# Cross attention of a two-layer transformer block: four of eight query chunks between its steps

## The chip, the cores and the metric

The kernel runs on one core of one Trainium2 chip. The core has TensorE (matmul, PE in the profile), VectorE (DVE), ScalarE (ACT), GpSimd (POOL) and SyncE (SP, which issues the DMAs here), each with its own in-order queue, synchronised by semaphores. The metric is the device time of one execution in microseconds.

## The reference, cut to what matters

Two layers, each a mixer of four branches, then cross attention to 256 memory rows, then a gated feed-forward part. `x` is 512 x 1024. The part that matters:

```
def memory_cross_attention(h, mem, mem_norm, wq, wk, wv, wo):
    m = rmsnorm(mem, mem_norm)
    q = (h @ wq).reshape(b, s, 4, 256)
    k = (m @ wk).reshape(b, -1, 4, 256)
    v = (m @ wv).reshape(b, -1, 4, 256)
    sc = einsum('bshd,bmhd->bhsm', q, k) * 256 ** -0.5
    p = softmax(sc, axis=-1)
    o = einsum('bhsm,bmhd->bshd', p, v).reshape(b, s, 1024)
    return o @ wo

x = x + memory_cross_attention(rmsnorm(x, norm_xa), mem, ...)
```

## The kernel before, in words

Activations lie transposed: 128 partitions of features, eight such tiles, 512 tokens along each. A weight matrix is cut into *chunks*: chunk n holds 128 output features of all 1024 inputs. A chunk is loaded as float32 into `raw`, ScalarE rounds it into `wh` (helper `hi(n)`), VectorE takes the rest `raw - wh` into `wl` (helper `lo(n)`), and TensorE multiplies it (helper `gemm`): for each of eight input tiles three fast matmuls of 512 columns, wh with the high part of the activation, wh with its low part, wl with the high part. `raw`, `wh`, `wl` and the PSUM banks `G` have two places each, by n modulo 2. So `hi(n)` waits until chunk n - 2 has been multiplied (`g_full`), `lo(n)` waits for `hi(n)`, `gemm(n)` waits for `lo(n)` and until the bank was emptied by the eviction of chunk n - 2, and SyncE's load of chunk n waits for `lo(n - 2)`.

Chunks N_WQ to N_WQ + 7 make the queries. VectorE evicts each into `qx` (L1289). Their input is the normed `x`, in `a_hi` and `a_lo`. Two query chunks belong to one head.

Cross attention then runs in 11 steps t, each engine through its own loop. Head t // 2, query half t % 2:

- TensorE, t < 8: scores of 256 queries against `kx` in plain float32 (L1716). It first waits until the head's second query chunk is evicted, and for t >= 2 until both exponentials of step t - 2 are done (`e_done` at `48 + 2 * (t - 1)`), which frees the bank.
- VectorE: negated row maximum (L1294), later the reciprocal of the sums (L1298) and the scaling of the exponentials (L1301).
- ScalarE: two exponentials with their sums (L817).
- TensorE, 2 <= t < 10: transposes ("turn") of the probabilities of step t - 2 (L1725); ScalarE copies them into `pt0` or `pt1` (L823).
- TensorE, t = 4, 6, 8, 10: the two output products of head t // 2 - 2, from `vx` and `pt` (L1428, `xo0` to `xo7`); ScalarE and VectorE split them into `b_hi` and `b_lo` (L827, L1306).

Then chunks N_WO to N_WO + 7 (the output projection) follow. No planner is at work: the order in every queue is the order in which the code stands. In VectorE's part the order behind a query chunk is fixed by these lines, the split of the chunk after next ahead of the eviction:

```
lo(n + 2)
...
dve.wait_ge(g_full, n + 1)
dve.scalar_tensor_tensor(qx[:, i, :], G[slot(n % 2)], C_XA, rbc[:], ALU.mult, ALU.mult).then_inc(g_dve, 1)
```

`pt0` and `pt1` lie over the 16 KB of `a_lo`, which nothing reads once the queries are made (L243, L244); `km` (the MLA branch's joined keys, 8 KB) is read by that branch's scores earlier in the layer.

Of the kernel before, what the change touches and what calls it, by code (L numbers as in the profile page):

```python
# [20 lines left out]
F32 = mybir.dt.float32  # L21
# [7 lines left out]
P = 128  # L29
D = 1024  # L30
S = 512
L = 2
KT = D // P
# [16 lines left out]
N_IN, N_WK, N_WV, N_OUT, N_WQ, N_WO, N_UP = 0, 15, 23, 31, 39, 47, 55  # L50
# [74 lines left out]
BIAS_AFTER.update({N_WK - 1 + u: (u,) for u in range(4, 16)})  # L125


def maps_at(t):

    return ([("diff", t, 0), ("diff", t, 1)] if t < 16 else []) + ([("mla", t - 1, 0)] if 1 <= t < 17 else [])  # L130
# [42 lines left out]
def block_program(nc, xT, memT, pos, const, vecs, small, w_first, w_main, w_up, w_down, w_last, out):  # L173
    with ExitStack() as ctx:
# [17 lines left out]
        def sb(name, shape, dt, at=None):  # L192
            size = (2 if dt == BF16 else 4) * int(np.prod(shape[1:]))
            if at is None:
                at = top[0]
                top[0] += (size + 31) // 32 * 32
                assert top[0] <= start + arena_bytes, (name, top[0] - start)
            return nc.alloc_sbuf_tensor_at(name, shape, dt, offset=at), at

        x_sb, _ = sb("x_sb", [P, KT, S], F32)  # L200
        a_hi, a_at = sb("a_hi", [P, KT, S], F32R)
        a_lo, _ = sb("a_lo", [P, KT, S], F32R)
        b_hi, bh_at = sb("b_hi", [P, KT, S], F32R)
        b_lo, bl_at = sb("b_lo", [P, KT, S], F32R)
        mask, _ = sb("mask", [P, 4, S], BF16)
        raw, _ = sb("raw", [P, 2, KT * P], F32)
        wh, _ = sb("wh", [P, 2, KT, P], F32R)
        wl, _ = sb("wl", [P, 2, KT, P], F32R)
        cst, _ = sb("cst", [P, NCC], F32)
        vec, _ = sb("vec", [P, NV], F32)  # L210
        sw, _ = sb("sw", [P, NSW], F32)
        rbc, _ = sb("rbc", [P, S], F32)
        rtmp, _ = sb("rtmp", [P, S], F32)
        rope, _ = sb("rope", [P, S], F32)
        ssum, ssum_at = sb("ssum", [P, S], F32)
        sqx, _ = sb("sqx", [P, 2, S], F32)
        mins, _ = sb("mins", [P, 48], F32)
        sums, _ = sb("sums", [P, 64], F32)
        rec, _ = sb("rec", [P, 64], F32)
        thin, _ = sb("thin", [P, len(ROOTS), 8], F32)  # L220
        xneg, _ = sb("xneg", [P, 16], F32)
        lqk, _ = sb("lqk", [P, 2, 32], F32)
        fvec, _ = sb("fvec", [P, 8], F32)
        lam, _ = sb("lam", [P, 8], F32)
# [15 lines left out]

        mems, _ = sb("mems", [P, KT, 2, M], F32R, a_at)
        memh, meml = mems[:, :, 0, :], mems[:, :, 1, :]
        pt0, _ = sb("pt0", [P, 4, S], F32, a_at + 16384)  # L243
        pt1, _ = sb("pt1", [P, 4, S], F32, a_at + 24576)  # L244
        pt = [pt0, pt1]
        dring, _ = sb("dring", [P, 8, S], F32, a_at + 16384)
        psa, _ = sb("psa", [P, 528], F32, kx_at + 4096)
# [93 lines left out]
        def layer_program(layer):  # L341
# [194 lines left out]
            def scalar(act):  # L536
# [268 lines left out]
                hi(N_WQ + 2)  # L805
                roots("stat_xa", c("eps6"), 1.0 / D)
                row_of("stat_xa")
                for n in range(N_WQ + 1, N_WO):
                    hi(n + 2)

                for t in range(11):
                    if t < 8:
                        act.wait_ge(xmax, t + 1)
                        act.wait_ge(t_full, 32 + t - 3 if t >= 4 else 32)
                        for q in range(2):
                            k = 2 * t + q
                            act.activation(ering[:, t % 4, M * q:M * q + M], SC[t % 2][:, M * q:M * q + M], ACT.Exp,  # L817
                                           bias=xneg[:, k:k + 1], accum_out=sums[:, 48 + k:49 + k]).then_inc(e_done, 1)
                    if 2 <= t < 10:
                        u = t - 2  # L820
                        act.wait_ge(t_full, 32 + u + 1)
                        act.wait_ge(v_full, V_AT[("diff1", "diff1", "xo1", "xo3")[u // 2]] + 1)
                        act.activation(pt[u // 2 % 2][:, 0:2, M * (u % 2):M * (u % 2) + M],  # L823
                                       TR[u % 2].rearrange("p (k q) -> p k q", k=2), ACT.Copy).then_inc(t_free, 1)
                    if t >= 4 and t % 2 == 0:
                        for i in range(t - 4, t - 2):
                            act.activation(b_hi[:, i, :], v_wait(f"xo{i}"), ACT.Copy).then_inc(o_hi, 1)  # L827
# [64 lines left out]
            def vector(dve):  # L892
# [386 lines left out]
                        lo(N_OUT + i + 2)  # L1279
                    split_x(i, mix, v("g_xa", i))  # L1280

                for i in range(KT):
                    n = N_WQ + i
                    lo(n + 2)
                    if i == 0:
                        inverse("stat_xa")
                        row_in("stat_xa")
                    dve.wait_ge(g_full, n + 1)
                    dve.scalar_tensor_tensor(qx[:, i, :], G[slot(n % 2)], C_XA, rbc[:], ALU.mult, ALU.mult).then_inc(g_dve, 1)  # L1289

                for t in range(11):
                    if t < 8:
                        dve.wait_ge(s_full, 48 + t + 1)
                        dve.tensor_reduce(xneg[:, 2 * t:2 * t + 2], SC[t % 2].rearrange("p (q m) -> p q m", q=2),  # L1294
                                          AX.X, ALU.max, negate=True).then_inc(xmax, 1)
                        k = 48 + 2 * t
                        dve.wait_ge(e_done, k + 2)
                        step(dve.reciprocal(rec[:, k:k + 2], sums[:, k:k + 2]))  # L1298
                        for q in range(2):
                            e = ering[:, t % 4, M * q:M * q + M]  # L1300
                            ins = dve.tensor_scalar(e, e, rec[:, k + q:k + q + 1], None, ALU.mult)  # L1301
                        ins.then_inc(p_ready, 1)
                    if t >= 4 and t % 2 == 0:
                        for i in range(t - 4, t - 2):
                            dve.wait_ge(o_hi, i + 1)
                            dve.tensor_tensor(b_lo[:, i, :], v_wait(f"xo{i}"), b_hi[:, i, :].bitcast(F32),  # L1306
                                              ALU.subtract).then_inc(v_dve, 1)
# [73 lines left out]
            def tensor(pe):  # L1381
# [23 lines left out]
                def gemms(base, count, his, los, tokens, free, tiles=range(KT), lead=0):  # L1405

                    turns = (count - lead) // 4 if count - lead > 6 else 0
                    for s in range(lead, count - 4 * turns):
                        gemm(base + s, (base + s) % 2, his, los, tokens, free, tiles)
                    if turns:  # L1410
                        at = base + count - 4 * turns
                        with pe.Fori(0, turns) as j:
                            for s in range(4):
                                gemm(j * 4 + at + s, (at + s) % 2, his, los, tokens, free, tiles)
# [285 lines left out]
                gemm(N_WQ + 1, 0, a_hi, a_lo, free="wq", tiles=range(4), end=False)  # L1700
                row_of("stat_xa")
                gemm(N_WQ + 1, 0, a_hi, a_lo, tiles=range(4, KT), begin=False)
                gemms(N_WQ, KT, a_hi, a_lo, S, "wq", lead=2)

                for t in range(11):
                    if t < 8:
                        h, qp = t // 2, t % 2
                        pe.wait_ge(g_dve, g_dve_count(N_WQ + 2 * h + 1, "wq"))
                        if t >= 2:
                            pe.wait_ge(e_done, 48 + 2 * (t - 1))  # L1710
                        else:
                            pe.wait_ge(s_seen, 48)
                        for q in range(2):
                            at = (2 * qp + q) * P
                            for i in range(2):
                                last = pe.matmul(SC[t % 2][:, M * q:M * q + M], qx[:, 2 * h + i, at:at + P],  # L1716
                                                 kx[:, 2 * h + i, :], start=(i == 0), stop=(i == 1))
                        last.then_inc(s_full, 1)
                    if 2 <= t < 10:
                        u = t - 2  # L1720
                        pe.wait_ge(p_ready, 16 + u + 1)
                        pe.wait_ge(t_free, 32 + u - 1)
                        for q in range(2):
                            for m in range(2):
                                last = pe.transpose(TR[u % 2][:, M * m + P * q:M * m + P * q + P],  # L1725
                                                    ering[:, u % 4, M * q + P * m:M * q + P * m + P], ident)
                        last.then_inc(t_full, 1)
                    if t >= 4 and t % 2 == 0:
                        h = t // 2 - 2
                        pe.wait_ge(t_free, 32 + 2 * h + 2)  # L1730
                        for i in range(2):
                            product(f"xo{2 * h + i}", *[(vx[:, m, GW * h + P * i:GW * h + P * i + P],
                                                         pt[h % 2][:, m, :]) for m in range(2)])

                gemm(N_WO, 1, b_hi, b_lo, free="wo",
                     ready=lambda i: pe.wait_ge(v_dve, V_FREED["dve"].index(f"xo{i}") + 1))
# [203 lines left out]
```

## Time and profile before

| | us |
|---|---|
| median of 3 runs (lowest, highest) | 1634.95 (1634.67, 1635.6) |
| the profiled execution, its own time | 1632.93 |
| its span, first to last instruction | 1631.1 |
| TensorE matmuls busy | 1580.3 |
| VectorE busy | 1009.3 |
| ScalarE busy | 729.4 |
| GpSimd busy | 166.7 |
| mean granted clock of TensorE, as a share of 2.4 GHz | 0.986 |

The span lies inside the execution's own time; the remaining 1.8 us are before and after it. Busy times of engines overlap, so they do not add up to the span. Matmuls are pipelined: one that is shown with 0.39 us is followed by the next after 0.23 us, so prices are read from one start to the next.

### The profile page before, as it was taken

What the parts mean: (1) busy time and instruction counts of PE and PEld (TensorE: products, weight loads), DVE (VectorE), ACT (ScalarE), POOL (GpSimd) and SP (SyncE); (2) the same over time, 40 slices, a digit from 0 to 9 for tenths busy, and PEclk for the clock granted to TensorE, in tenths of its full rate; (3) what the DMA queues carried; (4) which work ended last, traced back from release to release, by engine and by line L of the source; (5) the groups of instructions that cost most, each with busy time, mean ns of one, the idle gap of its engine ahead of it and who ended that gap; (6) DMA issues with size and microseconds to landing.
All of it is one profiled execution on the core that took longest, in us unless ns stands there. A gap on an engine that the chain in (4) does not pass through costs nothing.

```text
span 1631.1 us, 21918 instructions
## 1 busy us (share of the span) xinstructions
PE 1580.3 (97%) x7934; PEld 1236.5 (76%) x7934; DVE 1009.3 (62%) x1565; ACT 729.4 (45%) x1137; POOL 166.7 (10%) x114
## 2 busy tenths in 40 slices
PE   6999899999999999999999999999999999999997
PEld 3774677687688888888888677768768888888886
DVE  6785976443447746745767997654344773674574
ACT  5785667432444423423453266743244441442342
POOL 0000024220030000000021402422003000000002
PEclk9998999999999999999999999999999999999998
DMA  5321432122022223232233133212202223222222
GB/s 185 117 91 46 149 104 98 52 91 91 13 91 95 98 91 103 90 104 90 90 141 114 65 104 110 98 52 91 91 13 91 103 90 103 91 103 91 98 82 91
DMA packets 45438, 151.31 MB, mean 93 GB/s; under 512 B 5040, under 2 KB 5296, under 8 KB 44720
## 3 DMA queue, kind: packets, MB, share of 16 engines
q1 hardware_dynamic: 45360, 150.24, 26.6%
q8 instruction: 53, 0.87, 0.2%
q14 instruction: 25, 0.20, 0.0%
HBM read 142.88 MB, written 7.34 MB: 92 GB/s over the span
## 4 chain that ended last, share of the span: by engine, by line
PE 91%; DVE 5%; ACT 2%; issue 1%; DMA 1%; SPq 0%; DVEq 0%; ACTq 0%
PE psum L1395 25%; PE psum L1397 25%; PE psum L1398 25%; PE psum L1428 4%; PE psum L1583 2%; PE psum L1594 2%; PE psum L1561 2%; PE psum L1569 2%; PE psum L1463 1%; PE psum L1437 1%; PE psum L1449 1%; DVE wl L899 1%; ACT wh L543 1%; DVE acc L941 1%; PE psum L1716 1%
## 5 line engine op out<-in xcount | busy, mean ns | idle before, releaser
L543 ACT ACTIVATE wh<-raw 128x1024 fp32r<-128x1024 f32 x226 | 239.4, 1059 | 577.5 <-PE psum L1398 563.8
L1395 PE MATMUL psum<-a_hi,wh 128*128 128x512 f32 x1072 | 426.0, 397 | 0.8 <-DVE a_lo L964 0.6
L1397 PE MATMUL psum<-a_lo,wh 128*128 128x512 f32 x1072 | 419.8, 392 | 0.0
L1398 PE MATMUL psum<-a_hi,wl 128*128 128x512 f32 x1072 | 419.5, 391 | 0.0
L899 DVE TENSOR_TENSOR wl<-raw,wh 128x1024 fp32r<-128x1024 f32 x222 | 272.7, 1228 | 128.7 <-ACT wh L543 128.5
L1395 PE MATMUL psum<-b_hi,wh 128*128 128x512 f32 x608 | 240.9, 396 | 8.2 <-DVE x_sb L1273 4.4
L1395 PEld LDWEIGHTS psum<-a_hi,wh 128*128 128x128 f32 x1072 | 203.1, 189 | 51.0 <-issue 5.4
L1398 PE MATMUL psum<-b_hi,wl 128*128 128x512 f32 x608 | 237.6, 391 | 0.0
L1397 PE MATMUL psum<-b_lo,wh 128*128 128x512 f32 x608 | 237.3, 390 | 0.0
L1398 PEld LDWEIGHTS psum<-a_hi,wl 128*128 128x128 f32 x1072 | 202.8, 189 | 42.9
L1397 PEld LDWEIGHTS psum<-a_lo,wh 128*128 128x128 f32 x1072 | 203.1, 189 | 42.3 <-issue 1.2
L1273 DVE TENSOR_TENSOR x_sb<-x_sb,psum 128x512 f32<-128x512 f32 (+1 forms) x80 | 54.9, 686 | 180.2 <-PE psum L1398 180.2
L1395 PEld LDWEIGHTS psum<-b_hi,wh 128*128 128x128 f32 x608 | 114.6, 188 | 37.6 <-issue 6.5
L1397 PEld LDWEIGHTS psum<-b_lo,wh 128*128 128x128 f32 x608 | 114.6, 188 | 24.0 <-issue 1.0
L1398 PEld LDWEIGHTS psum<-b_hi,wl 128*128 128x128 f32 x608 | 114.4, 188 | 24.2
L925 DVE TENSOR_TENSOR up<-psum,rbc 128x512 f32<-128x512 f32 x88 | 60.9, 692 | 89.2 <-PE psum L1398 84.5
L941 DVE SCALAR_TENSOR_TENSOR acc<-conv_in,vec,acc 128x512 f32<-128x512 f32 x120 | 95.6, 797 | 3.4
L517 POOL TENSOR_TENSOR ssum<-ssum,sqx 128x512 f32<-128x512 f32 x41 | 73.1, 1784 | 128.7 <-ACT sqx L566 128.7
L1395 PE MATMUL psum<-mems,wh 128*128 128x256 f32 x256 | 81.3, 318 | 0.0
L504 POOL TENSOR_TENSOR wl<-raw,wh 128x1024 fp32r<-128x1024 f32 x20 | 47.9, 2393 | 322.2 <-ACT wh L543 320.9
L514 POOL COPY ssum<-sqx 128x512 f32<-128x512 f32 x6 | 4.3, 719 | 720.3 <-ACT sqx L566 720.3
L1397 PE MATMUL psum<-mems,wh 128*128 128x256 f32 x256 | 72.7, 284 | 0.0
(223 smaller groups left out, 1953.3 us busy)
## 6 DMA issues: line engine op xcount, KB each, us to landing
raw<-in_w_main SPq DMA_DIRECT2D x106, 512.0 KB, 3.2
raw<-in_w_up SPq DMA_DIRECT2D x88, 512.0 KB, 3.2
raw<-in_w_down SPq DMA_DIRECT2D x32, 512.0 KB, 3.2
raw<-in_w_last SPq DMA_DIRECT2D x16, 384.0 KB, 3.0
bias_scratch<-ptr SPq DMA_DIRECT2D x16, 256.0 KB, 2.8
bias<-bias_scratch SPq DMA_DIRECT2D x16, 256.0 KB, 3.8
sw<-in_small SPq DMA_DIRECT2D x2, 1152.0 KB, 6.3
raw<-in_w_first SPq DMA_DIRECT2D x4, 512.0 KB, 4.9
```

The source lines that it names most:

```text
L504: pool.tensor_tensor(wl[:, slot(n % 2)].rearrange("p k m -> p (k m)"), raw[:, slot(n % 2), :], wh[:, slot(n % 2)].rearrange("p k m -> p (k ...
L517: pool.tensor_tensor(ssum[:], ssum[:], sqx[:, k % 2, :], ALU.add).then_inc(ss_in, 1)
L543: act.activation(wh[:, slot(b)].rearrange("p k m -> p (k m)")[:, 0:width], raw[:, slot(b), 0:width], ACT.Copy).then_inc(w_hi, 1)
L899: dve.tensor_tensor(wl[:, slot(b)].rearrange("p k m -> p (k m)"), raw[:, slot(b), :], wh[:, slot(b)].rearrange("p k m -> p (k m)").bitcast ...
L925: dve.tensor_tensor(dst, G[slot(b)], rbc[:], ALU.mult).then_inc(g_dve, 1)
L941: ins = dve.scalar_tensor_tensor(acc[:, i, :], win, w, acc[:, i, :], ALU.mult, ALU.add)
L1273: dve.tensor_tensor(x_sb[:, at, :], x_sb[:, at, :], G[slot(b)].rearrange("p (o s) -> p o s", o=1), ALU.add).then_inc(g_dve, 1)
L1395: pe.matmul(out_ap, wh[:, slot(b), k, :], his[:, k, :], start=((begin or first) and i == 0), stop=False)
L1397: pe.matmul(out_ap, wh[:, slot(b), k, :], los[:, k, :], start=False, stop=False)
L1398: last = pe.matmul(out_ap, wl[:, slot(b), k, :], his[:, k, :], start=False, stop=(end and i == len(tiles) - 1))
L1428: last = pe.matmul(ps[rows, cols], lhs, rhs, start=(i == 0), stop=(i == len(pairs) - 1))
L1561: pe.matmul(SC[m], qk[rows, h // 2, qb * P:qb * P + P], qk[rows, 2 + h // 2, :], start=True, stop=True).then_inc(s_full, 1)
```

## The change

The queries' first four chunks are multiplied as before, ahead of the attention steps. The last four stand in the steps: TensorE multiplies query chunk 4 at the end of step 2, 5 at the end of step 3, 6 at the end of step 4, 7 at the end of step 5. ScalarE's conversion of the chunk after next and VectorE's split and eviction stand at the beginning of steps 3, 4, 5 and 6. Because `a_hi` and `a_lo` are now read until step 5, `pt0` and `pt1` (which use only two of their four planes) shrink to two planes each and lie over `km`.

```diff
--- before.py
+++ after.py
@@ -123,6 +123,10 @@
 STORES_AHEAD = {n: (n - 4,) for n in range(4, 16)}
 STORES_AHEAD.update({16: (12, 13, 14), 17: (15,)})
 BIAS_AFTER.update({N_WK - 1 + u: (u,) for u in range(4, 16)})
+
+
+
+XA_CHUNKS = {3: 4, 4: 5, 5: 6, 6: 7}
 
 
 def maps_at(t):
@@ -240,8 +244,8 @@
 
         mems, _ = sb("mems", [P, KT, 2, M], F32R, a_at)
         memh, meml = mems[:, :, 0, :], mems[:, :, 1, :]
-        pt0, _ = sb("pt0", [P, 4, S], F32, a_at + 16384)
-        pt1, _ = sb("pt1", [P, 4, S], F32, a_at + 24576)
+        pt0, _ = sb("pt0", [P, 2, S], F32, km_at)
+        pt1, _ = sb("pt1", [P, 2, S], F32, km_at + 4096)
         pt = [pt0, pt1]
         dring, _ = sb("dring", [P, 8, S], F32, a_at + 16384)
         psa, _ = sb("psa", [P, 528], F32, kx_at + 4096)
@@ -805,10 +809,12 @@
                 hi(N_WQ + 2)
                 roots("stat_xa", c("eps6"), 1.0 / D)
                 row_of("stat_xa")
-                for n in range(N_WQ + 1, N_WO):
+                for n in range(N_WQ + 1, N_WQ + 4):
                     hi(n + 2)
 
                 for t in range(11):
+                    if t in XA_CHUNKS:
+                        hi(N_WQ + XA_CHUNKS[t] + 2)
                     if t < 8:
                         act.wait_ge(xmax, t + 1)
                         act.wait_ge(t_full, 32 + t - 3 if t >= 4 else 32)
@@ -1279,7 +1285,8 @@
                         lo(N_OUT + i + 2)
                     split_x(i, mix, v("g_xa", i))
 
-                for i in range(KT):
+                def queries(i):
+
                     n = N_WQ + i
                     lo(n + 2)
                     if i == 0:
@@ -1288,7 +1295,12 @@
                     dve.wait_ge(g_full, n + 1)
                     dve.scalar_tensor_tensor(qx[:, i, :], G[slot(n % 2)], C_XA, rbc[:], ALU.mult, ALU.mult).then_inc(g_dve, 1)
 
+                for i in range(4):
+                    queries(i)
+
                 for t in range(11):
+                    if t in XA_CHUNKS:
+                        queries(XA_CHUNKS[t])
                     if t < 8:
                         dve.wait_ge(s_full, 48 + t + 1)
                         dve.tensor_reduce(xneg[:, 2 * t:2 * t + 2], SC[t % 2].rearrange("p (q m) -> p q m", q=2),
@@ -1700,7 +1712,8 @@
                 gemm(N_WQ + 1, 0, a_hi, a_lo, free="wq", tiles=range(4), end=False)
                 row_of("stat_xa")
                 gemm(N_WQ + 1, 0, a_hi, a_lo, tiles=range(4, KT), begin=False)
-                gemms(N_WQ, KT, a_hi, a_lo, S, "wq", lead=2)
+                gemm(N_WQ + 2, 1, a_hi, a_lo, free="wq")
+                gemm(N_WQ + 3, 0, a_hi, a_lo, free="wq")
 
                 for t in range(11):
                     if t < 8:
@@ -1731,6 +1744,9 @@
                         for i in range(2):
                             product(f"xo{2 * h + i}", *[(vx[:, m, GW * h + P * i:GW * h + P * i + P],
                                                          pt[h % 2][:, m, :]) for m in range(2)])
+                    if t + 1 in XA_CHUNKS:
+                        i = XA_CHUNKS[t + 1]
+                        gemm(N_WQ + i, (N_WQ + i) % 2, a_hi, a_lo, free="wq")
 
                 gemm(N_WO, 1, b_hi, b_lo, free="wo",
                      ready=lambda i: pe.wait_ge(v_dve, V_FREED["dve"].index(f"xo{i}") + 1))
```

## Rows read from the trace of the kernel before

**Rows 1.** The page: busy time of TensorE, and the weight loads (size, us to landing).

```profile
PE 1580.3 (97%) x7934; PEld 1236.5 (76%) x7934; DVE 1009.3 (62%) x1565; ACT 729.4 (45%) x1137; POOL 166.7 (10%) x114
...
raw<-in_w_main SPq DMA_DIRECT2D x106, 512.0 KB, 3.2
```

**Rows 2.** Windows of the stage: length, busy us and instructions of each engine, granted clock (PEclk).

```profile
399.88:436.28 36.40, 32.16 (x130) 21.30 (x128) 17.70 (x41) 18.35 (x49) 0.00 (x0) 1.00 0.04 15
424.05:436.28 12.23, 10.04 (x38) 5.67 (x36) 4.15 (x9) 4.87 (x11) 0.00 (x0) 1.00 0.00 1
1172.65:1209.04 36.39, 32.15 (x130) 21.29 (x128) 17.70 (x41) 18.35 (x49) 0.00 (x0) 1.00 0.04 15
```

**Rows 3.** Timeline of TensorE, first layer: start, us, then idle before it and its releaser.

```profile
399.88 3.61 PE L1716 MATMUL psum<-kx,qx 128*128 128x256 f32 x16
404.84 1.97 PE L1716 MATMUL psum<-kx,qx 128*128 128x256 f32 x8 [1.35 <-ACT ering L817]
406.65 0.60 PE L1725 MATMUL psum<-cst,ering 128*128 128x128 f32 x4
...
416.29 1.89 PE L1716 MATMUL psum<-kx,qx 128*128 128x256 f32 x8
418.01 0.60 PE L1725 MATMUL psum<-cst,ering 128*128 128x128 f32 x4
418.45 1.89 PE L1716 MATMUL psum<-kx,qx 128*128 128x256 f32 x8
...
420.62 3.60 PE L1428 MATMUL psum<-pt,vx 128*128 128x512 f32 x8
424.05 1.89 PE L1716 MATMUL psum<-kx,qx 128*128 128x256 f32 x8
...
428.26 3.70 PE L1428 MATMUL psum<-pt,vx 128*128 128x512 f32 x8 [1.45 <-ACT pt L823]
...
436.28 0.80 PE L1395 MATMUL psum<-b_hi,wh 128*128 128x512 f32 x1
```

**Rows 4.** Timelines of ScalarE and VectorE behind the last query chunk, first layer.

```profile
394.69 1.06 ACT L543 ACTIVATE wh<-raw 128x1024 fp32r<-128x1024 f32 x1 [4.38 <-PE psum L1398]
400.13 1.06 ACT L543 ACTIVATE wh<-raw 128x1024 fp32r<-128x1024 f32 x1 [4.38 <-PE psum L1398]
...
401.22 1.22 DVE L899 TENSOR_TENSOR wl<-raw,wh 128x1024 fp32r<-128x1024 f32 x1 [3.61 <-ACT wh L543]
402.37 0.68 DVE L1289 SCALAR_TENSOR_TENSOR qx<-psum,rbc 128x512 f32<-128x512 f32 x1
402.96 0.68 DVE L1294 TENSOR_REDUCE xneg<-psum 128x2 f32<-128x512 f32 x1
```

**Rows 5.** Windows over gaps of TensorE elsewhere, and over what followed them.

```profile
129.20:132.50 3.30, 0.00 (x0) 0.00 (x0) 0.69 (x1) 3.24 (x4) 0.00 (x0) 1.00 0.46 174
133.50:147.20 13.70, 13.70 (x37) 3.60 (x37) 4.82 (x8) 0.00 (x0) 0.00 (x0) 0.50 0.01 1
195.30:197.50 2.20, 0.00 (x0) 0.00 (x0) 2.16 (x5) 0.01 (x1) 0.00 (x0) 1.00 0.60 212
198.40:201.80 3.40, 3.40 (x17) 3.24 (x15) 3.33 (x8) 1.92 (x5) 0.00 (x0) 0.50 0.00 0
321.30:324.70 3.40, 3.40 (x9) 2.62 (x9) 2.69 (x4) 2.08 (x3) 1.91 (x2) 0.51 0.30 116
1092.30:1094.50 2.20, 0.01 (x2) 0.04 (x1) 1.89 (x3) 0.69 (x3) 0.00 (x0) 1.00 0.00 0
1096.00:1100.00 4.00, 4.00 (x19) 3.34 (x18) 2.38 (x3) 1.77 (x3) 2.16 (x2) 1.00 0.36 125
```

**Rows 6.** Timeline around one such gap, at the start of the output chunks.

```profile
319.28 0.68 DVE L1273 TENSOR_TENSOR x_sb<-x_sb,psum 128x512 f32<-128x512 f32 x1
...
320.11 0.48 PE L1395 MATMUL psum<-b_hi,wh 128*128 128x512 f32 x1 [2.20 <-DVE x_sb L1273]
...
320.42 0.40 PE L1397 MATMUL psum<-b_lo,wh 128*128 128x512 f32 x1
```

## Prediction

> **What bounds the kernel now.** I read the page first: TensorE's matmuls are busy 97% of the span [rows 1]. A change that adds no arithmetic can therefore only win where TensorE waits or where its clock is down, and it loses wherever it makes TensorE wait. Then I read the stage that the diff touches, from the first cross-attention score to the first matmul of the output projection: 36.40 us in the first layer and 36.39 us in the second, all at granted clock 1.00 [rows 2]. The two copies agree, so I work out one layer and double it.
>
> The timeline of TensorE through the stage [rows 3] gives the price of each piece by differences of starts. A step's scores take 418.01 - 416.29 = 1.72 us, its transposes ("turn") 418.45 - 418.01 = 0.44 us, a pair of output products 424.05 - 420.62 = 3.43 us. Eight scores, eight turns and four pairs make 31.0 us, so TensorE idles 5.4 us here. Three parts: 1.35 us before the scores of step 2, which wait for the first exponentials; small gaps from step 2 to step 6, where the chain maximum, exponential, reciprocal takes longer than the matmuls; and the tail after the scores of step 7, 12.23 us long, with 1.45 us of its wait in one row.
>
> How much is in the middle part? From the turn in step 2 (406.65) to the scores of step 7 (424.05) are 17.40 us. The matmuls there are five turns, four scores and two pairs: 2.20 + 6.88 + 6.86 = 15.94 us. The gaps are 1.46 us.
>
> **What the change moves.** Four query chunks of 24 matmuls leave the front of the stage and stand at the ends of steps 2, 3, 4 and 5. A chunk costs 400.13 - 394.69 = 5.44 us of TensorE, read from one weight conversion to the next [rows 4]; 4 x 5.44 = 21.76 us stand in both kernels and cancel. The opening stays: scores 0 and 1, the split and eviction behind the last chunk, the table load and the 1.35 us wait follow chunk 3 as they followed chunk 7. The tail stays too: the last chunk is over before step 6, and between scores 6 and scores 7 stand the same turn and pair. Nothing fills the 1.45 us there.
>
> **What it wins.** From step 3 on each score finds its exponentials done, since a chunk of 5.44 us stands before it. All the middle gaps go: -1.46 us a layer. The cover holds even though ScalarE and VectorE now do a weight conversion, a weight split and an eviction before the maximum of steps 3 and 5. That maximum starts about 3.1 us after its chunk's end (402.96 against 399.88 for the same three pieces in the old order [rows 3, 4]) and its probabilities are ready some 2.6 us later, 5.7 us in all; TensorE has scores, turn and the next chunk to do, 1.72 + 0.44 + 5.44 = 7.6 us.
>
> **What it costs: two waits.** The scores of steps 4 and 5 belong to head 2, which reads query chunks 4 and 5. The wait in front of step 4 asks for chunk 5 evicted, and chunk 5 is the very last thing TensorE did, at the end of step 3. The same holds for chunk 7 before step 6. Chunks 4 and 6 are not wanted at once and cost nothing. What lies between the end of a chunk and its eviction is seen behind chunk 7 of the old order [rows 4]: ScalarE converts the weights of the chunk after next (it has to wait for this chunk, whose buffer it overwrites) from 400.13, VectorE splits them from 401.22, and only then, because `lo(n + 2)` stands ahead of the eviction in `queries`, the eviction runs from 402.37 to 403.05. In the old order this was hidden behind scores 0 and 1 (3.44 us), which read other chunks. Now nothing is behind the waiting scores but what they must precede: TensorE's queue is in order, so the turn, the pair and the next chunk wait too.
>
> The size: TensorE's next slot would be 399.88 [rows 3]; the eviction ends at 403.05; from the end of a VectorE instruction to the matmul that it frees are 320.11 - (319.28 + 0.68) = 0.15 us [rows 6]. So 403.20 - 399.88 = 3.32 us, and the first matmul after an idle stretch takes 0.31 us to its successor [rows 6] instead of a chunk's usual 5.44 / 24 = 0.23, 0.08 us. That is 3.40 us a wait, 6.80 us a layer.
>
> **Small terms.** Each chunk now follows other matmul forms and may pay that same 0.08 us again: between 0 and 0.32 us a layer; I take 0.32, the nearest row. The number of instructions of every engine is the same; the loop of chunks was already written out. SyncE's weight loads keep their order and come later with the splits that free their buffers: a load lands in 3.2 us [rows 1] and is issued behind the split of two chunks before, which is at least 8 us ahead of the conversion that reads it (two chunks less the 2.5 us of conversion and split), so 0. GpSimd has nothing in this stage. The turned tiles `pt0` and `pt1` move to the place of `km`, last read in the maps before; they keep their waits, so 0.
>
> Per layer: 6.80 + 0.32 - 1.46 = +5.66 us; two layers +11.3 us.
>
> **The clock.** These are gaps of over 3 us, which the stage did not have. Elsewhere the trace has four gaps of 2.2 to 3.3 us in the middle of work [rows 5, 6]. After an idle 2.2 us the granted clock fell to 0.50 (1.2 of 2.4 GHz) at 198.4 for 3.4 us; after an equal one that ended at 320.1 it fell at 321.3 for 3.4 us; after 3.3 us of idle it fell for 13.7 us, in products that partly use half the rows; a third gap of 2.2 us, at 1092.3, did not bring it down. So three of four fell, the longest among them. I take three of my four waits to be followed by one such stretch. A stretch costs half of 3.4 us, 1.7 us, since dense matmuls stand behind both waits: +5.1 us. The bounds are nothing, and for all four two stretches each, 13.6 us.
>
> The Trainium skill, "TensorE: Matmul & The Clock Gate", section "HAM oscillation", says that waits between bursts of matmuls bring the array back to the lower clock and that every following burst then starts slow. By that rule all four waits would be followed by a slow stretch and the clock term would be 6.8 us, for a sum of +18.1 us. The trace agrees in three gaps of four.
>
> **The sum.** +11.3 + 5.1 = +16.4 us. The profiled execution took 1632.93 us (span 1631.1), which would become 1649.3; the median of the runs shown is 2.0 us above it, and 1634.95 + 16.4 = 1651.4 us is my forecast, 1.0% slower.
>
> **The rivals.**
> *The waits are there, the clock holds.* For it: the gap at 1092.3 left the clock at 1.00. Against it: my gaps are half again as long. +11.3 us, 1646.3 us, down to 1645.2 without the small term and with 0.1 us less a wait. Chance 0.2.
> *The clock stays down longer.* For it: the 13.7 us stretch; scores, turn and pair behind the wait are plain fp32 as the products there were. Against it: those products partly used 64 rows, and in the other two cases one stretch was enough. Two stretches behind each wait: 11.3 + 13.6 = +24.9 us, 1659.9 us. Chance 0.09.
> *The eviction is not held back by the split.* If the wait were only chunk end to eviction, 0.25 + 0.68 + 0.15 + 0.08 = 1.16 us, the layer would be 2.32 + 0.32 - 1.46 = +1.2 us, and the kernel 1637.3 us, within 0.2%. Against it stands the order in `queries` and the row of the split. Chance 0.05.
> *The gaps are filled and no new wait opens* (the other side). This asks that the evictions of chunks 5 and 7 are done when the scores come. It decides below (1.46 - 0.32) / 2 = 0.57 us a wait. With none, the layer wins 1.14 us: 1632.7 us, still within 0.2%; only with the opening wait and the tail filled too (5.4 us of idle less 0.32, twice) could it reach -10.2 us, 1624.8 us. For it: the gaps are real and a chunk is long enough. Against it: chunks 5 and 7 directly precede their readers, and neither opening nor tail is touched. Chance 0.06, half of it faster.
>
> **How the numbers follow.** Forecast 0.60, for one to four ordinary slow stretches (1648.0 to 1653.1 us); clock holds 0.20; longer stretches 0.09; small wait 0.05; no wait 0.06. The range runs from the clock-holds case, with a microsecond below it, to just short of the case of two stretches everywhere: 1644 to 1659 us. It leaves out the two unslowed cases and the far end of the long stretches, some 0.15. A measurement of this kernel tells 0.2%, 3.3 us, from no change. Faster 0.03, within 0.2% 0.07, slower 0.90.
>
> **What the profile after would show.** Right: two rows in each layer where the scores wait over 3 us for VectorE's `qx`, a stage from first score to output projection of 36.4 + 21.8 + 5.7 = 63.8 us plus clock losses, no wait at steps 3 and 5, the same tail, and a clock of 0.50 behind most waits. Wrong: a wait near 1 us would mean that the split does not hold the eviction back; waits at steps 3 or 5 that my cover of 7.6 us was miscounted; a tail shorter than 12.2 us that I missed what the new order does late.

## The result, and the profile after

| | before | after |
|---|---|---|
| median, us | 1634.95 | 1649.31 |
| lowest to highest of 5 runs, us | 1631.89 to 1637.43 | 1646.89 to 1650.88 |
| ratio to before, 95% interval | | 1.0096 (1.0085 to 1.0108) |
| profiled execution (span), us | 1632.93 (1631.1) | 1650.88 (1649.1) |

The changed kernel is about 1% slower; the forecast was 1651.4 us. From the page of the changed kernel, the row that answers to [rows 1]: the same 7934 matmuls, 7.0 us more of recorded busy time.

```profile
PE 1587.3 (96%) x7934; PEld 1240.1 (75%) x7934; DVE 1015.3 (62%) x1565; ACT 729.9 (44%) x1137; POOL 163.9 (10%) x114
```

Windows of the changed kernel answer to [rows 2]: the stage from the first score to the first output matmul, in both layers, and the tail of the first from the scores of step 7. The columns are those of [rows 2].

```profile
379.17:444.37 65.20, 55.52 (x225) 40.22 (x224) 25.08 (x49) 22.74 (x53) 0.00 (x0) 0.97 0.12 41
1159.03:1225.94 66.91, 57.23 (x225) 41.38 (x224) 25.10 (x49) 22.80 (x53) 0.00 (x0) 0.95 0.12 40
432.15:444.37 12.22, 10.03 (x37) 5.66 (x36) 4.03 (x8) 4.87 (x11) 0.00 (x0) 1.00 0.00 0
```

The stage now holds four chunks more, 21.76 us. Against 36.40 and 36.39 us it grew by 28.80 and 30.52 us, so it lost 7.04 and 8.76 us, 15.8 us together, of 18.0 us between the two profiled spans. The tail is 12.22 us, as before (12.23). Where the 15.8 us are is seen in the timeline of TensorE, which answers to [rows 3]; the chunks' own matmuls are left out.

```profile
379.17 3.61 PE L1729 MATMUL psum<-kx,qx 128*128 128x256 f32 x16
384.14 1.97 PE L1729 MATMUL psum<-kx,qx 128*128 128x256 f32 x8 [1.36 <-ACT ering L823]
385.94 0.60 PE L1738 MATMUL psum<-cst,ering 128*128 128x128 f32 x4
...
391.85 1.89 PE L1729 MATMUL psum<-kx,qx 128*128 128x256 f32 x8
...
402.71 1.99 PE L1729 MATMUL psum<-kx,qx 128*128 128x256 f32 x8 [3.07 <-DVE qx L1296]
...
413.89 1.89 PE L1729 MATMUL psum<-kx,qx 128*128 128x256 f32 x8
...
424.76 3.55 PE L1729 MATMUL psum<-kx,qx 128*128 128x256 f32 x8 [3.07 <-DVE qx L1296]
428.10 0.77 PE L1738 MATMUL psum<-cst,ering 128*128 128x128 f32 x4
428.71 3.60 PE L1440 MATMUL psum<-pt,vx 128*128 128x512 f32 x8
432.15 1.89 PE L1729 MATMUL psum<-kx,qx 128*128 128x256 f32 x8
...
436.36 3.70 PE L1440 MATMUL psum<-pt,vx 128*128 128x512 f32 x8 [1.45 <-ACT pt L829]
```

The middle gaps are gone: nothing waits before the scores at 391.85 (step 3) and 413.89 (step 5). Two waits of 3.07 us took their place, at 402.71 (step 4) and 424.76 (step 6), both released by VectorE's `qx`. What VectorE did before the first of them answers to [rows 4]:

```profile
400.83 1.23 DVE L905 TENSOR_TENSOR wl<-raw,wh 128x1024 fp32r<-128x1024 f32 x1 [3.31 <-ACT wh L547]
401.97 0.68 DVE L1296 SCALAR_TENSOR_TENSOR qx<-psum,rbc 128x512 f32<-128x512 f32 x1
404.75 0.69 DVE L1306 TENSOR_REDUCE xneg<-psum 128x2 f32<-128x512 f32 x1 [2.09 <-PE psum L1729]
```

It splits weights from 400.83, evicts chunk 5 from 401.97 to 402.65, and TensorE starts at 402.71. The next slot after chunk 5 would have been at 399.49 (its last matmul started at 399.26), so the wait is 3.22 us long. The view of waits, over both layers, adds the four up:

```profile
PE psum L1729 <- DVE qx L1296: 12.3, 4, 3.1
```

The scores at 424.76 took 3.55 us where eight usually take 1.89. That is the granted clock, in these windows behind the four waits:

```profile
402.70:406.00 3.30, 3.29 (x15) 2.55 (x16) 0.69 (x1) 0.53 (x3) 0.00 (x0) 1.00 0.44 159
425.10:428.50 3.40, 3.40 (x11) 2.65 (x10) 0.15 (x1) 0.00 (x0) 0.00 (x0) 0.51 0.47 159
1183.00:1186.00 3.00, 3.00 (x8) 2.25 (x7) 0.00 (x0) 0.00 (x0) 0.00 (x0) 0.50 0.50 175
1206.80:1210.10 3.30, 3.30 (x11) 2.57 (x10) 0.27 (x1) 0.00 (x0) 0.00 (x0) 0.50 0.45 159
```

Three of four waits were followed by a stretch at 0.50 to 0.51, 1.2 of 2.4 GHz; the first wait of the first layer was not.

Outside the stages 2.2 us remain. Half of it is in front of the first stage, which would begin at 378.12 if only four chunks had left and begins at 379.17; the other half is in the last rows of the program. There VectorE's last residual and its first output stood 6.78 us apart in the changed kernel, 5.78 before, with only small matmuls between them:

```profile
1634.27 0.69 DVE L1279 TENSOR_TENSOR x_sb<-x_sb,psum 128x512 f32<-128x512 f32 x1 [3.39 <-PE psum L1410]
...
1641.05 5.35 DVE L1819 SCALAR_TENSOR_TENSOR x_sb<-x_sb,vec,psum 128x512 f32<-128x512 f32 x8 [2.23 <-PE psum L1461]
```

```profile
1617.34 0.69 DVE L1273 TENSOR_TENSOR x_sb<-x_sb,psum 128x512 f32<-128x512 f32 x1 [3.39 <-PE psum L1398]
...
1623.12 5.36 DVE L1803 SCALAR_TENSOR_TENSOR x_sb<-x_sb,vec,psum 128x512 f32<-128x512 f32 x8 [1.90 <-PE psum L1449]
```

The change has nothing in either place; the clock was down at other moments there. In front of the stage the granted clock was 0.51 from 35.9 to 42.8 us (0.75 before), 0.81 from 98 to 107 us (0.62 before) and 0.54 from 131 to 149.5 us (0.63 before). At the end it fell to 0.50 at 1636.8 us, half way through the small matmuls; before it fell at 1621.8 us, in their last group.

### The profile page after: what moved, and what is told of

The parts are those of the page before. It is cut to its first block, busy times and chain, and to the rows that moved or that the text cites. A ratio compares the mean times of both kernels' runs of the same rounds, so it can differ in the third digit from the quotient of the medians.

```text
span 1649.1 us, 21918 instructions
## 1 busy us (share of the span) xinstructions
PE 1587.3 (96%) x7934; PEld 1240.1 (75%) x7934; DVE 1015.3 (62%) x1565; ACT 729.9 (44%) x1137; POOL 163.9 (10%) x114
## 4 chain that ended last, share of the span: by engine, by line
PE 91%; DVE 5%; ACT 2%; issue 1%; DMA 1%; SPq 0%; DVEq 0%; ACTq 0%
PE psum L1407 25%; PE psum L1410 24%; PE psum L1409 24%; PE psum L1440 4%; PE psum L1595 2%; PE psum L1606 2%; PE psum L1573 2%; PE psum L1729 2%; PE psum L1581 2%; DVE wl L905 1%; PE psum L1475 1%; PE psum L1449 1%; ACT wh L547 1%; PE psum L1461 1%; DVE acc L947 1%
## 5 line engine op out<-in xcount | busy, mean ns | idle before, releaser
L1410 PEld LDWEIGHTS psum<-a_hi,wl 128*128 128x128 f32 x1072 | 202.6, 189 | 42.8
```

The costliest lines, as they stand in the source:

```text
L1410: last = pe.matmul(out_ap, wl[:, slot(b), k, :], his[:, k, :], start=False, stop=(end and i == len(tiles) - 1))
```

## The experiments

One theory stood against three rivals. Theory W: the loss is two waits a layer, each the length of conversion, split and eviction of a chunk that the very next scores read, and a slow clock behind most of them. The rivals: the place of the tiles costs (M), interleaving costs in itself (I), the clock costs nothing and the waits are all of it (C). All kernels were timed against the kernel before on the same chip; those of the first four experiments shared one chip, the next three another, the last two a third. The median of before was 1634.66, 1633.21 and 1633.5 us on these chips.

**The tiles moved, nothing else.**

```diff
-        pt0, _ = sb("pt0", [P, 4, S], F32, a_at + 16384)
-        pt1, _ = sb("pt1", [P, 4, S], F32, a_at + 24576)
+        pt0, _ = sb("pt0", [P, 2, S], F32, km_at)
+        pt1, _ = sb("pt1", [P, 2, S], F32, km_at + 4096)
```

> The kernel before with one half of the change alone: the turned tiles pt0 and pt1 lie over km, the order of all queues is as before. Theory W (two waits per layer of some 3.2 us in front of the scores of steps 4 and 6, and a slow clock behind most of them) expects no change: within 0.2% of 1635 us, a stage of 36.4 us in each layer. Rival M (the place of the tiles costs: ScalarE's copies into them or the output products that read them are slower there) expects the copies above 0.60 us or the products' pairs above 3.43 us, and part of the 14 us lost.

1635.13 us, ratio 1.0003 (0.9991 to 1.0015). The stages, as windows:

```profile
399.76:436.17 36.41, 32.16 (x130) 21.31 (x128) 17.70 (x41) 18.36 (x49) 0.00 (x0) 1.00 0.05 16
1174.15:1210.56 36.41, 32.16 (x130) 21.30 (x128) 17.70 (x41) 18.35 (x49) 0.00 (x0) 1.00 0.05 15
```

ScalarE's copies into `pt` took 0.59 us each, as in the kernel before. This half of the change costs nothing; rival M is out.

**The eviction ahead of the split**, for the four moved chunks of the changed kernel:

```diff
-                    lo(n + 2)
+                    if not evict_first:
+                        lo(n + 2)
...
                     dve.scalar_tensor_tensor(qx[:, i, :], ...).then_inc(g_dve, 1)
+                    if evict_first:
+                        lo(n + 2)
...
-                        queries(XA_CHUNKS[t])
+                        queries(XA_CHUNKS[t], evict_first=True)
```

> The changed kernel, with the eviction of the four moved chunks ahead of the weight split in VectorE's queue. Theory W expects the two waits per layer to fall from an idle of 3.07 us to about 0.8 us (0.25 to VectorE's start, 0.68 for the eviction, 0.06 to TensorE, less the 0.16 us that a matmul's record outlasts its slot), some 2.25 us less each, and the slow clock behind them to vanish: 1649.3 - 4 x 2.25 - 5 = about 1635.5 us, the same as the kernel before. Rival I (interleaving itself costs, by switches between matmul forms and by ScalarE and VectorE being late everywhere) expects it to stay above 1645 us.

1634.36 us, ratio 1.0007 (0.9994 to 1.0020). VectorE's timeline before step 4, first layer, and the two waiting scores of that layer in TensorE's:

```profile
399.74 0.69 DVE L1297 SCALAR_TENSOR_TENSOR qx<-psum,rbc 128x512 f32<-128x512 f32 x1 [2.75 <-PE psum L1413]
400.89 1.23 DVE L905 TENSOR_TENSOR wl<-raw,wh 128x1024 fp32r<-128x1024 f32 x1 [0.46 <-ACT wh L547]
```

```profile
400.49 1.99 PE L1732 MATMUL psum<-kx,qx 128*128 128x256 f32 x8 [0.78 <-DVE qx L1297]
...
420.24 1.99 PE L1732 MATMUL psum<-kx,qx 128*128 128x256 f32 x8 [0.78 <-DVE qx L1297]
```

The stages of both layers, as windows:

```profile
379.20:438.17 58.97, 53.86 (x225) 39.08 (x224) 25.47 (x49) 22.66 (x53) 0.00 (x0) 1.00 0.14 46
1155.30:1214.27 58.97, 53.86 (x226) 39.07 (x224) 25.47 (x49) 22.66 (x53) 0.00 (x0) 1.00 0.14 45
```

One exchange of two instructions on VectorE gives back all of the loss that can be measured. The waits are 0.78 us each instead of 3.07, and the granted clock is 1.00 through both stages. The stage takes 58.97 us, 0.8 us more than the 58.16 us of the old order with four chunks in it (36.40 + 21.76): the short waits cost a little more than the filled gaps give, too little for the medians to show. Rival I is out: the chunks are still between the steps. The Trainium skill, "TensorE: Matmul & The Clock Gate", section "Architectural detail: the array is 16× 32×32, not 1× 128×128", says that VectorE and ScalarE take their instructions strictly in order. The trace agrees: in the changed kernel the eviction, whose input was ready at the chunk's end (399.49), ran only behind the split, at 401.97; here it ran at 399.74.

**Each moved chunk one step earlier.**

```diff
-XA_CHUNKS = {3: 4, 4: 5, 5: 6, 6: 7}
+XA_CHUNKS = {2: 4, 3: 5, 4: 6, 5: 7}
```

> The changed kernel with each moved chunk one step earlier (ends of steps 1, 2, 3 and 4), so that chunks 5 and 7 have a whole step between them and the scores that read them. Theory W expects no wait for the evictions at all, and also the opening wait of 1.36 us filled, as a chunk now stands in front of the scores of step 2: per layer 1.46 + 1.36 + 0.08 saved less up to 0.2 for switches, so the stage is 58.16 - 2.7 = 55.4 us from the first score with four chunks in it, and the kernel is 5.4 us faster than before, about 1629.5 us. Rival I expects it slower than before, above 1640 us.

1628.97 us, ratio 0.9971 (0.9960 to 0.9981): faster than before. Scores of steps 0 and 1, 2, 5 and 6 in the first layer:

```profile
375.83 3.61 PE L1729 MATMUL psum<-kx,qx 128*128 128x256 f32 x16
...
384.75 1.89 PE L1729 MATMUL psum<-kx,qx 128*128 128x256 f32 x8
...
411.10 1.89 PE L1729 MATMUL psum<-kx,qx 128*128 128x256 f32 x8
...
414.33 1.99 PE L1729 MATMUL psum<-kx,qx 128*128 128x256 f32 x8 [0.91 <-DVE qx L1296]
```

The opening wait of 1.36 us is gone, but not every wait for `qx`: 0.91 us stand before step 6 (the timeline's x8 rows at 384.75 and 411.10 have no wait). That part of the expectation was wrong. Step 5 holds no chunk, only 2.16 us of scores and turn, less than the 3.2 us from the end of chunk 7 to the first matmul that its eviction frees. The stage was 56.42 us (375.83 to 432.25) against 58.16 for the old order with four chunks, 55.4 expected. So the two stages account for 3.5 us. That the median came out 5.7 us below that of before, where 5.4 was expected, is partly luck. The profiled execution has a span 4.7 us shorter than before, 1.2 us of it outside the stages: the clock stayed at 1.00 from 198.4 to 203.3 us and from 321.3 to 326.1 us, where it had fallen in the trace of before [rows 5].

**The wait filled.** The changed kernel, with matmuls whose result is overwritten unread:

```diff
+                        if t in (4, 6):
+                            pe.wait_ge(w_lo, N_WQ + t + 3)
+                            pe.wait_ge(e_done, 48 + 2 * (t - 1))
+                            for _ in range(13):
+                                pe.matmul(SC[0], wh[:, slot((N_WQ + t + 2) % 2), 0, :], a_hi[:, 0, :],
+                                          start=True, stop=True)
                         pe.wait_ge(g_dve, g_dve_count(N_WQ + 2 * h + 1, "wq"))
```

> The changed kernel with 13 matmuls of 512 columns, whose result is overwritten unread, in front of each of the two waits per layer: 2.95 us of work in a wait of 3.2 us, so that the wait keeps its length in time and only the idleness goes. Theory W with its clock term expects the four waits to be as long as before and the granted clock at 1.00 behind them: 1649.3 - 5.1 (three slow stretches of 1.7 us) = about 1644.5 us, the waits alone being worth 10.4. Rival C (the clock term is nothing, all 14 us are the waits) expects 1649.3 us, within 0.1%.

1643.75 us (1642.82 to 1644.05), ratio 1.0056 (1.0040 to 1.0073). TensorE around the first wait, then the stages of both layers and the windows behind the two waits of the first:

```profile
397.39 3.11 PE L1725 MATMUL psum<-a_hi,wh 128*128 128x512 f32 x13
400.63 1.99 PE L1734 MATMUL psum<-kx,qx 128*128 128x256 f32 x8
```

```profile
377.06:440.62 63.56, 59.77 (x251) 43.95 (x250) 25.09 (x49) 22.67 (x53) 0.00 (x0) 1.00 0.13 42
1155.31:1218.87 63.56, 59.76 (x251) 43.95 (x250) 25.09 (x49) 22.68 (x53) 0.00 (x0) 1.00 0.13 42
400.60:404.00 3.40, 3.37 (x15) 2.59 (x16) 0.69 (x1) 0.61 (x3) 0.00 (x0) 1.00 0.47 154
422.70:426.00 3.30, 3.30 (x15) 2.57 (x16) 0.69 (x1) 0.55 (x3) 0.00 (x0) 1.00 0.45 159
```

The scores start 3.24 us after the chunk (400.63 against 397.39), so the wait is as long as it was, and only the idleness is gone. The clock is 1.00 through the stage, which takes 63.56 us in both layers: 5.40 us lost a layer. The changed kernel's 65.20 and 66.91 us are 5.0 us more together, one slow stretch in the first layer (1.64) and two in the second (3.35). The medians, 1649.31 and 1643.75 us, differ by 5.6 us, though they were not measured side by side. Rival C is out. The Trainium skill, "TensorE: Matmul & The Clock Gate", section "HAM oscillation — how this bites in real kernels", has idle waits between bursts of matmuls bring the clock down, if they are long enough. The trace agrees as far as idleness goes: the same wait of 3.2 us, filled with work, left the clock at 1.00.

**Chunks 4 and 5 one step earlier, 6 and 7 left.**

```diff
-XA_CHUNKS = {3: 4, 4: 5, 5: 6, 6: 7}
+XA_CHUNKS = {2: 4, 3: 5, 5: 6, 6: 7}
```

> The changed kernel with chunks 4 and 5 one step earlier (ends of steps 1 and 2), chunks 6 and 7 left at the ends of steps 4 and 5. A dose test: theory W expects the wait before step 4 gone and the one before step 6 whole, idle 3.07 us, with its slow clock in about three of four cases. The stage with its four chunks: 58.16 - 1.36 - 0.08 - 1.46 + 3.3 + 0.1 = 58.7 us a layer at full clock, so 1634.7 + 1.1 + 2 x 0.75 x 1.7 = about 1638 us, between one step earlier (1629.0) and the changed kernel (1649.3). Rival I (the loss comes from chunks between the steps as such) expects 1645 us or more.

1640.36 us, ratio 1.0041 (1.0029 to 1.0054): between its neighbours, but 2 us above the expectation. The scores of steps 4 and 6, first layer, and the windows behind the long wait in each layer:

```profile
399.21 1.99 PE L1729 MATMUL psum<-kx,qx 128*128 128x256 f32 x8 [0.91 <-DVE qx L1296]
...
421.26 3.42 PE L1729 MATMUL psum<-kx,qx 128*128 128x256 f32 x8 [3.07 <-DVE qx L1296]
```

```profile
422.20:425.50 3.30, 3.30 (x11) 2.54 (x11) 0.69 (x1) 0.05 (x1) 0.00 (x0) 0.56 0.34 129
1197.00:1203.60 6.60, 6.20 (x15) 4.44 (x16) 1.60 (x5) 1.51 (x5) 0.00 (x0) 0.52 0.24 79
```

The same miscount: chunk 5 now ends step 2, step 3 holds no chunk, and 0.91 us stay uncovered before step 4, 1.8 us in the two layers. That makes up most of the 2 us above the expectation. The long wait is whole, and the clock fell in both layers, in the second to 0.52 over 6.6 us.

**One step earlier and the eviction first** (the edits of the second and third experiments together).

> One step earlier, and the eviction ahead of the split. One step earlier left a wait of 0.91 us before the scores of step 6: chunk 7 ends step 4, and step 5 has only 1.72 + 0.44 = 2.16 us of scores and turn to cover 3.2 us. With the eviction first, 0.95 us are to be covered by 2.16. Theory W expects no wait for qx at all, a stage of 56.42 - 0.99 = 55.4 us, and 1629.0 - 2 = about 1627 us. If the split put behind the eviction delays something else (the maximum of the same step), the stage stays at 56.4 us.

1628.58 us, ratio 0.9971 (0.9957 to 0.9986), where about 1627 us was expected. The scores and the products of step 6:

```profile
414.58 1.89 PE L1732 MATMUL psum<-kx,qx 128*128 128x256 f32 x8
...
417.19 3.70 PE L1443 MATMUL psum<-pt,vx 128*128 128x512 f32 x8 [0.28 <-ACT pt L829]
```

No wait for `qx` remains; 0.28 us before the products took part of its place, since the split still precedes the maximum of step 5, and with it the exponentials and the copy of the turned tiles. The stage is 55.80 us (377.15 to 432.95), 0.6 better than one step earlier alone and 0.4 short of the 55.4 expected; the medians do not tell the two kernels apart.

**The tail filled, at the wrong place.** Into the kernel of the last experiment (one step earlier, eviction first). An eighth of a chunk is the three matmuls of one input tile:

```diff
                         pe.wait_ge(t_free, 32 + 2 * h + 2)
+                        if t in (8, 10):
+                            gemm(N_WO, 1, b_hi, b_lo, ..., end=False, tiles=range(2) if t == 8 else range(2, 3), ...)
...
-                gemm(N_WO, 1, b_hi, b_lo, free="wo",
+                gemm(N_WO, 1, b_hi, b_lo, tiles=range(3, KT), begin=False,
```

> The kernel before this one, and in addition two eighths of the first output chunk ahead of the output products of step 8 and one eighth ahead of those of step 10, where TensorE waits 1.45 and 0.74 us for the copies of the turned tiles. Expected: those waits fall to nearly nothing, 2.0 us a layer, about 1623 us. The rival: the three eighths need the first outputs' splits and the weights of the output chunk, which are ready (the split of the third output ends before step 8), so no new wait; if one appears it is put in front of the products, and the gain is less than 2 us a layer.

1627.25 us, ratio 0.9967 (0.9952 to 0.9981), hardly better; 1623 was expected. TensorE's timeline shows why:

```profile
424.86 0.50 PE L1410 MATMUL psum<-b_hi,wh 128*128 128x512 f32 x1 [1.45 <-ACT pt L829]
...
431.13 0.50 PE L1410 MATMUL psum<-b_hi,wh 128*128 128x512 f32 x1 [0.74 <-ACT pt L829]
```

The waits for `pt` stayed whole and only changed their owner: the eighths stood ahead of the products but behind the products' wait. What the expectation asked for needs them ahead of the wait, and the edit did not do that.

**The same ahead of the wait** (the new lines moved above `pe.wait_ge(t_free, ...)`), and **that alone in the kernel before**.

> The tail filled once more, this time with the three eighths of the first output chunk ahead of TensorE's wait for the turned tiles; in the kernel before this one they stood behind that wait, in front of the products, so the waits of 1.45 and 0.74 us stayed whole. Two eighths are 6 x 0.227 = 1.36 us against 1.45, one eighth 0.68 us against 0.74. Expected: waits of some 0.1 us left, the stage from first score to the last eighths 2.0 us shorter in each layer less up to 0.2 for a matmul's first slot after another form, 1628.6 - 3.8 = about 1625 us. If the eighths delayed the products instead, the stage would stay as it was.

> The kernel before with only that filling of the tail, the query chunks all at the front. Expected: 3.8 us faster than before, about 1630.5 us, since the tail is the same in every version (12.2 us from the scores of step 7 to the output chunk). If the gain of filling depended on the chunks between the steps, this would show less.

With the other edits 1625.30 us, ratio 0.9945 (0.9931 to 0.9960); alone 1627.88 us, ratio 0.9964 (0.9949 to 0.9978). The first of the two:

```profile
424.44 0.48 PE L1410 MATMUL psum<-b_hi,wh 128*128 128x512 f32 x1
...
426.14 3.70 PE L1443 MATMUL psum<-pt,vx 128*128 128x512 f32 x8
...
430.03 0.48 PE L1410 MATMUL psum<-b_hi,wh 128*128 128x512 f32 x1
...
431.02 3.70 PE L1443 MATMUL psum<-pt,vx 128*128 128x512 f32 x8
```

The eighths run while the copies are made, and the products at 426.14 and 431.02 show no wait. In both kernels the traces give 2.04 us a layer, the three eighths that now cost nothing. Alone, the time from the first score to the chunk's fourth eighth is 36.40 us (397.37 to 433.77), as long as the stage of before up to the first eighth; with the other edits it is 55.80 us (378.35 to 434.15), as long as in the kernel without the filling. So the filling is worth what it replaces, with or without chunks between the steps. The median of the filling alone lies 5.6 us below that of before, for 4.1 us shown in the two stages; the interval holds both. 1625.3 us is the best version seen, 0.55% faster than before.

## Why the prediction was right

**The two waits.** Right in place, cause and number. Forecast 3.32 us and 0.08 us for the first matmul; measured 3.22 and 0.11 (402.71 to 404.54 is 1.83, usual 1.72). The 0.1 us by which the wait was forecast too long is the step from VectorE to TensorE: 0.06 us from 402.65 to 402.71, not the 0.15 of [rows 6]. That the eviction's place behind conversion and split makes up most of it was shown by the eviction put first: 0.78 us of idle in place of 3.07.

**The gaps won.** Right: no wait at steps 3 and 5, and the tail and the opening unchanged.

**The switches.** Over-sized. The slot from the turn's end to the scores of step 3 is 391.85 - 385.94 - 0.44 = 5.47 us, 0.03 more than a chunk alone, where 0.08 was taken for each chunk.

**The sum at full clock.** Forecast +5.66 us a layer. The filled wait, where the clock did not fall, measured +5.40.

**The clock.** Forecast three stretches of 1.7 us, and the profiled execution had three, 5.0 us by the stage windows. That it was exactly three is partly luck: the number was taken from four gaps and could have been two or four in this execution. The higher term of 6.8 us, a slow stretch behind every wait, would have been too much here: one wait of the four left the clock at 1.00. Over all kernels with waits of 3.07 us (changed kernel and the one with chunks 4 and 5 early) five of six were followed by a low clock; of the eight waits of 0.78 and 0.91 us, in the traces of the three kernels that have them, none was.

**The sum.** +16.4 us forecast, +14.4 us by the medians, +18.0 us by the two profiled spans: 10.8 for the waits less the filled gaps, 5.0 for the clock in the stages, and 2.2 outside the stages, which the forecast did not have. That the forecast lies between the two is no proof of each term; the terms rest on the trace and on the two experiments above. The forecast said 1% slower and it is 0.96%.

**The rivals.** That the clock holds would have needed 1646.3 us or a little less. All five runs lie above that, the lowest by only 0.6 us; the windows at 0.50 and the filled wait decide it. That the clock stays down for two stretches behind every wait (1659.9 us) did not happen in the changed kernel: each of the three was a single one. It can happen: one wait of the kernel with chunks 4 and 5 early had 6.6 us at 0.52. That the eviction is not held back would have been 1637.3 us, 2.4 us above before; the exchange of the two instructions makes that case true, and its two stages took 1.6 us more than those of before (ratio 1.0007, nothing that the runs can tell apart). That no new wait opens (1632.7 us) is refuted by the two waits, and that case is what the last kernels bring about: with the opening and the tail filled as well, the best of them is 8.2 us faster than before, where the prediction put the bound at 10.2. The view that any interleaving costs (rival I of the experiments) is refuted by the two early versions, which interleave and are faster.

## What to carry to other kernels

A chunk of work put into a gap must not be the producer of what the very next instruction reads. Count the whole path from its last matmul to the consumer, with everything that stands ahead of the eviction in the other engine's in-order queue, and count what really lies in the step between, not "a step". When a wait cannot be avoided, the drain should come first and the preparation of later work behind it: here that order alone was worth some 14 us, of which 5 us were the clock.

Filler belongs above the wait that it is to hide. Below it, the wait only changes its owner in the profile.

## What the runs showed of the hardware that was not expected

A gap of one and the same length brings the clock down in one execution and not in another. The gap of 2.2 us before the second layer's output chunks left the clock at 1.00 in the kernel before [rows 5]; in the kernel with only the tiles moved, whose instruction order is the same, it was followed by this window:

```profile
1095.90:1099.10 3.20, 3.20 (x9) 2.46 (x9) 2.36 (x3) 1.74 (x3) 1.72 (x2) 0.51 0.25 78
```

The runs of the kernel before spread from 1629.57 to 1637.36 us on one chip, more than the 3.3 us that the prediction took for what a measurement tells from no change; its medians in the four comparisons agree to about 0.1%. The spread goes with the clock: of its 29 runs there the fastest had a mean granted clock of 0.988, and the four above 1637 us had 0.983 or 0.984. Since 0.001 of 1633 us is 1.6 us, this difference is an estimated 6.5 to 8 us, about the whole spread. Which gaps made it in which run, no trace shows. The six runs of the kernel with the filled waits had 0.985 or 0.986 and spread by 1.2 us; why their clock varied less is open. Their median lies 9.1 us above that of before where its two stages lost 10.8, but the two profiled spans, 1642.0 and 1631.1 us, differ by 10.9: the 1.7 us between are the median of before lying above its profiled execution.
